# A multi-layer trunk kernel on one core: the first modulation and the first projection block taken feature tile by feature tile, with new ring slots and a new order of the adaLN steps

## The reference

```python
def layer(x, cond, l, p, ctx):
    mod = jnp.einsum('...d,de->...e', jax.nn.silu(cond), p['w_ada'][l]) + p['b_ada'][l]
    sh1, sc1, g1, sh2, sc2, g2 = jnp.split(mod.reshape(-1, 1, 6 * D_MODEL), 6, axis=-1)
    hn = rmsnorm(x, p['norm_mix'][l]) * (1.0 + sc1) + sh1
    mix, ctx_tensors = token_mixers(hn, l, p, ctx)     # proj = hn @ w_in[l]: attention, retention, HGRN2
    x = x + g1 * mix                                   # mix ends in @ w_out[l]
    hn = rmsnorm(x, p['norm_ffn'][l]) * (1.0 + sc2) + sh2
    x = x + g2 * moe(hn, l, p)                         # 16 experts, two picked for each token
    return x, ctx_tensors
```

## Time and profile before

| | |
|---|---|
| median of three runs | 952.8 us |
| the profiled run, and its span | 953.32 us, 951.5 us |
| TensorE busy | 920.2 us (97%) |
| VectorE, ScalarE, POOL busy | 431.9, 158.7, 63.7 us |
| adaLN loads | 48 of 1024 KB |
| projection loads | 28 of 1024 KB, 4 of 512 KB |

### The profile page before, as it was taken

One profiled execution on the slowest core, in us unless ns is written; L12 is line 12 of the kernel. 1 busy time (PEld: TensorE's weight loads), 2 busy tenths in 40 slices (PEclk: granted clock), 3 DMA queues, 4 the chain that ended last, 5 costly groups with the idle time before them and its releaser, 6 DMA issues.

```text
span 951.5 us, 13385 instructions
## 1 busy us (share of the span) xinstructions
PE 920.2 (97%) x5191; PEld 499.6 (53%) x5197; DVE 431.9 (45%) x780; ACT 158.7 (17%) x408; POOL 63.7 (7%) x96
## 2 busy tenths in 40 slices
PE   5999999999999999999999999999999999999997
PEld 2755575568553444344437556657864444443442
DVE  1385887742423122232145999876252321222223
ACT  2212024320210100010111211432021001000100
POOL 1112230020000000000000223000000000000001
PEclk9999999999999999999999999999999999999999
DMA  9996574675999999999996632601189999999993
GB/s 365 401 390 268 222 267 177 243 278 213 408 420 422 421 421 421 421 422 420 421 421 252 225 124 91 235 32 38 35 364 422 421 421 421 421 421 421 421 421 137
DMA packets 48430, 303.63 MB, mean 319 GB/s; under 512 B 7680, under 2 KB 7696, under 8 KB 14960
## 3 DMA queue, kind: packets, MB, share of 16 engines
q1 hardware_dynamic: 42368, 291.52, 75.2%
q0 software_dynamic: 2960, 8.63, 2.6%
q10 hardware_dynamic: 3040, 2.62, 0.8%
HBM read 300.10 MB, written 2.65 MB: 318 GB/s over the span
## 4 chain that ended last, share of the span: by engine, by line
PE 84%; DVE 9%; DMA 3%; ACT 2%; issue 1%; SPq 0%; DVEq 0%; ACTq 0%
PE ps L427 82%; PE ps L461 2%; DMA ring<-in_w_in 2%; ACT eP L1582 1%; DMA ring<-in_w_ada 1%; DVE fa L1263 1%; DVE rt L1057 1%; DVE eP L1361 1%; DVE stat L1057 1%; DVE xy L1257 1%; DVE eP L1359 1%; DVE hnT L1105 0%; DVE sq L1214 0%; DVE proj L1290 0%; DVE proj L1224 0%
## 5 line engine op out<-in xcount | busy, mean ns | idle before, releaser
L427 PE MATMUL ps<-ring,proj 128*64 128x512 f32 x1024 | 226.3, 595 | 1.0 <-ACT proj L1829 1.0
L427 PE MATMUL ps<-ring,hnT 128*128 128x512 f32 (+1 forms) x576 | 203.2, 505 | 2.3 <-issue 1.2
L427 PEld LDWEIGHTS ps<-ring,hnT 128*128 128x128 f32 x576 | 106.9, 191 | 75.9 <-issue 67.7
L427 PEld LDWEIGHTS ps<-ring,proj 128*64 128x64 f32 x1024 | 72.6, 137 | 132.8 <-issue 131.1
L427 PE MATMUL ps<-hnT,ring 128*64 128x128 f32 (+2 forms) x576 | 74.0, 342 | 2.9 <-DVE hnT L1105 1.6
L427 PEld LDWEIGHTS ps<-hnT,ring 128*64 128x64 f32 (+1 forms) x576 | 60.7, 160 | 13.9 <-issue 2.9
L427 PEld LDWEIGHTS ps<-proj,xs 128*128 128x128 f32 x512 | 58.4, 192 | 12.5 <-issue 11.4
L427 PE MATMUL ps<-proj 128*128 128x512 f32 x128 | 61.7, 607 | 0.0
L427 PE MATMUL ps<-proj,xs 128*128 128x128 f32 x512 | 61.4, 278 | 0.1
L1553 DVE COPY proj<-ps 128x512 f32<-128x512 f32 x16 | 11.1, 692 | 108.0 <-PE ps L427 108.0
L427 PE MATMUL ps<-ring,silT 128*32 128x512 f32 x384 | 48.8, 630 | 9.6 <-DVE silT L1073 6.9
(11 more groups left out here) (231 smaller groups left out, 920.9 us busy)
## 6 DMA issues: line engine op xcount, KB each, us to landing
ring<-in_w_gate SPq DMA_DIRECT2D x64, 1024.0 KB, 14.4
ring<-in_w_down SPq DMA_DIRECT2D x64, 1024.0 KB, 16.8
ring<-in_w_ada SPq DMA_DIRECT2D x48, 1024.0 KB, 8.6
ring<-in_w_in SPq DMA_DIRECT2D x28, 1024.0 KB, 8.5
eP<-in_w_up SPq DMA_DIRECT2D x16, 1024.0 KB, 15.8
wT<-in_w_up SPq DMA_DIRECT2D x16, 1024.0 KB, 17.9
fa<-in_w_up SPq DMA_DIRECT2D x16, 1024.0 KB, 17.7
xy<-in_w_up SPq DMA_DIRECT2D x16, 1024.0 KB, 19.1
```

What stands on the lines that cost most here:

```text
L427: ins = nc.tensor.matmul(*a, **k)
```

## The change

- The x part of layer 0's w_ada is laid out anew on the host as `ada_x`: load k now has all 1024 rows, but only the 128 shift and 128 scale columns of feature tile k. Its sums are 8 multiplies of 256 columns, spread over four groups of 32 array columns (rows i and i + 4 share one); ScalarE copies the four partial rows, two tiny multiplies with `pick` add and turn them, VectorE makes shift and scale of this tile and applies them for g = 0, ScalarE for g = 1.
- Block f of layer 0 is computed along with it: for each k, 8 multiplies of 256 columns, into both banks, right after the sums of feature k + 1.
- f's two halves are loaded to slots 8 and 9 and stand before adaLN loads 1 and 4 in SyncE's order. The ring begins at slot 2, so that block b lies in slots 0 and 1, the six steps behind it in 2 to 7, and i in 0 and 1.
- SyncE issues conditioning, tokens and constants ahead of the weights; POOL keeps the small parameters.
- `ADA_BEHIND` of layer 0 goes from (2, 3, 3, 3, 3, 2, 3, 2) to (0, 0, 2, 6, 6, 2, 3, 2). Of the six behind b, TensorE does three after the first and three after the third quarter of b, none at its end.
- The diagonals of layer 0 move from before a's last quarter to the start of block b.
- VectorE clamps both banks of f before the gates of bank 0 in layer 0. Fourteen zero multiplies open TensorE's program and no longer wait for the conditioning.

The diff, cut:

```diff
-ADA_BEHIND = ((2, 3, 3, 3, 3, 2, 3, 2), (0, 0, 0, 0, 0, 3, 0, 0))
+ADA_BEHIND = ((0, 0, 2, 6, 6, 2, 3, 2), (0, 0, 0, 0, 0, 3, 0, 0))
 AT_CHANGE = 5
+ROWS_AHEAD = (1, 4)
+FIRST_SLOT = 2
...
+            n_loads = [FIRST_SLOT]
...
+            for name, dst, src in (("cond_dma", condT[:], ap["cond"]), ("x_dma0", x[:, 0], ap["x_prompt"][0]),
+                                   ("begin_dma", C["begin"][:], ap["begin"]), ("x_dma1", x[:, 1], ap["x_sample"][0])):
+                sp.dma_start(dst, src).then_inc(S(name), 16)
+                led.made(name, (name, 0), 16)
...
                 if l == 0:
-                    for step in EARLY:
-                        load_ada(*step)
+                    for k in range(KC):
+                        if k in ROWS_AHEAD:
+                            r = ROWS_AHEAD.index(k)
+                            load_rows(*IN_BLOCKS[0], r, RING + r)
+                        load(flat_slot, ap["ada_x"][k])
...
-            pe.wait_ge(c.of("silT"), c.at("silT"))
...
-                if l == 0:
-                    b = claim_for_norm()
-                    for step in EARLY[0:5]:
-                        ada_step(*step)
-                        stream_zeros(b, 3)
-                    pe.wait_ge(c.of("begin_dma"), c.at("begin_dma"))
-                    normalized_group("hn1", "xn1", 0, first=b)
-                    normalized_group("hn1", "xn1", 1)
-                    for step in EARLY[5:]:
-                        ada_step(*step)
-                    modulation_by_feature(0, 0)
-                else:
+                def sums_of_feature(k):
+
+                    pe.wait_ge(S("bank1_free"), c.claim(1))
+                    s = slot()
+                    for i in range(KC):
+                        q = slice(32 * (i % 4), 32 * (i % 4) + 32)
+                        last = mm(ps[q, 1, 0:2 * P], silT[:, i, :], by_k(s, 2 * P)[:, i] if i < KH else flat_slot(s)[:, 2 * P * i:2 * P * (i + 1)], start=i < 4, stop=i >= 4)
+                        if i < KC - 1:
+                            pay(last)
+                    last.then_inc(c.fills(1, "ada", 0, "x", k), 1)
+                    owed.append(s)
+
+                def modulation_of_feature(k):
+
+                    pe.wait_ge(S("bank7_free"), c.claim(7))
+                    pe.wait_ge(c.of("modX", 0, 0, k), c.at("modX", 0, 0, k))
+                    for a in range(2):
+                        last = mm(ps[:, 7, NG * a:NG * (a + 1)], modX[:, 2 * P * (k % 2) + P * a:2 * P * (k % 2) + P * (a + 1)], C["pick"], start=True, stop=True)
+                        if not a:
+                            pay(last)
+                    last.then_inc(c.fills(7, "modT", 0, 0, k), 1)
...
+                def feature_of_first_block(k, ss, banks):
+
+                    for g in range(NG):
+                        pe.wait_ge(c.of(f"hn1S{g}", k), c.at(f"hn1S{g}", k))
+                    for p in range(2):
+                        for hl in range(2):
+                            for d in range(2):
+                                col = 64 * (2 * p + hl) + 256 * d
+                                last = mm(ps[64 * d:64 * d + 64, banks[p], 256 * hl:256 * (hl + 1)], by_k(ss[k // KH], 512)[:, k % KH, col:col + 64], hnT[:, k, :], start=False, stop=(k == KC - 1), skip_group_check=True)
+                                if k == KC - 1 and hl and d:
+                                    last.then_inc(c.fills(banks[p], "projP", "f", p), 1)
+                                else:
+                                    pay(last)
+
+                if l:
...
+                if l:
+                    b = next_bank()
+                    ss = open_block("f")
+                    by_head_and_group("f", 0, ss, b)
+                    by_head("f", 1, ss)
+                else:
+                    f_banks = [next_bank() for _ in range(2)]
+                    pe.wait_ge(c.of("zero", 0), c.at("zero", 0))
+                    stream_zeros(f_banks[0], 12)
+                    stream_zeros(f_banks[1], 2)
+                    pe.wait_ge(c.of("begin_dma", 0), c.at("begin_dma", 0))
+                    normalized_group("hn1", "xn1", 0, banks=(4, 5))
+                    pe.wait_ge(c.of("silT"), c.at("silT"))
+                    sums_of_feature(0)
+                    normalized_group("hn1", "xn1", 1, banks=(6, 0))
+                    ss = []
+                    for k in range(KC):
+                        modulation_of_feature(k)
+                        if k + 1 in ROWS_AHEAD:
+                            ss.append(slot(RING + len(ss)))
+                        if k + 1 < KC:
+                            sums_of_feature(k + 1)
+                        feature_of_first_block(k, ss, f_banks)
+                        if k % KH == KH - 1:
+                            owed.append(ss[k // KH])
...
-                diagonal(0)
-                diagonal(1)
+                if l:
+                    diagonal(0)
+                    diagonal(1)
...
+                if not l:
+                    diagonal(0)
+                    diagonal(1)
                 for g in range(NG):
                     b = by_token("b", g, 0, ss)
+                    if not l:
+                        ada_steps(3)
...
-                ada_behind("b")
+                ada_steps(ADA_BEHIND[l][3] % 6)
...
+            st(v.memset(zero, 0.0), "zero", 0)
...
-                    modulation_by_feature(0, 0)
                     for k in range(KC):
-                        ins = ts(hnT[:, k, 0:P], hnT[:, k, 0:P], modT[:, 1, k, 0:1], modT[:, 0, k, 0:1], ALU.mult, ALU.add)
-                        if k % KH == KH - 1:
-                            ins.then_inc(c.makes("hn1S0", k // KH), 1)
+                        dve.wait_ge(c.of("modT", 0, 0, k), c.at("modT", 0, 0, k))
+                        tt(modTs[:, 0, 0:2, k], ps[:, 7, 0:2 * NG].rearrange("p (a g) -> p a g", a=2), badaTs[:, 0, 0:2, one(k)].broadcast_to([P, 2, NG]), ALU.add).then_inc(c.freed(("modT", 0, 0, k)), 1)
+                        dve.wait_ge(S(c.last[0]), c.last_value())
+                        st(stt(out=modTs[:, 0, 1, k], in0=modTs[:, 0, 1, k], scalar=1.0, in1=nrmTs[:, 0, 0, one(k)].broadcast_to([P, NG]), op0=ALU.add, op1=ALU.mult), "modS", 0, 0, k)
+                        ts(hnT[:, k, 0:P], hnT[:, k, 0:P], modT[:, 1, k, 0:1], modT[:, 0, k, 0:1], ALU.mult, ALU.add).then_inc(c.makes("hn1S0", k), 1)
...
-                gates(0)
+                bounded(0)
+                if l:
+                    gates(0)
+                    bounded(1)
+                else:
+                    bounded(1)
+                    gates(0)
...
+                            if not l:
+                                acte.wait_ge(c.of(f"x_dma{g}", 0), c.at(f"x_dma{g}", 0))
...
+                    evac(("ada", 0, "x", 0), None, "modX", 0, 0, 0, fn=lambda src: nc.scalar.copy(modX[:, 0:2 * P], src[:, 0:2 * P]))
                     for h in range(2):
                         evac(("hn1T", 1, h), None, fn=lambda src: nc.scalar.copy(hnT[:, KH * h:KH * (h + 1), P:2 * P], src.rearrange("p (k t) -> p k t", k=KH)))
-                    modulation(0, "x", 0)
-                    acte.wait_ge(c.of("modS", 0, 0), c.at("modS", 0, 0))
                     for k in range(KC):
-                        ins = act_(hnT[:, k, P:2 * P], hnT[:, k, P:2 * P], AF.Identity, bias=modT[:, 0, k, 1:2], scale=modT[:, 1, k, 1:2])
-                        if k % KH == KH - 1:
-                            ins.then_inc(c.makes("hn1S1", k // KH), 1)
+                        acte.wait_ge(c.of("modS", 0, 0, k), c.at("modS", 0, 0, k))
+                        act_(hnT[:, k, P:2 * P], hnT[:, k, P:2 * P], AF.Identity, bias=modT[:, 0, k, 1:2], scale=modT[:, 1, k, 1:2]).then_inc(c.makes("hn1S1", k), 1)
+                        if k + 1 < KC:
+                            to = modX[:, 2 * P * ((k + 1) % 2):2 * P * ((k + 1) % 2) + 2 * P]
+                            evac(("ada", 0, "x", k + 1), None, "modX", 0, 0, k + 1, fn=lambda src: nc.scalar.copy(to, src[:, 0:2 * P]))
...
-            for name, lot in (("cond_dma", [(condT[:], ap["cond"])]),
-                              ("begin_dma", [(x[:, 0], ap["x_prompt"][0]), (x[:, 1], ap["x_sample"][0]), (C["begin"][:], ap["begin"])]),
-                              ("mod_dma", [(mods[:], ap["mods"])])):
-                for dst, src in lot:
-                    pool.dma_start(dst, src).then_inc(S(name), 16)
-                led.made(name, (name,), 16 * len(lot))
+            pool.dma_start(mods[:], ap["mods"]).then_inc(S("mod_dma"), 16)
+            led.made("mod_dma", ("mod_dma",), 16)
...
+    first = np.asarray(inputs["w_ada"])[0, :, 0:2 * D].reshape(P, KC, 2, KC, P)
+    out["ada_x"] = first.transpose(3, 0, 1, 2, 4).reshape(KC, P, KC * 2 * P)
```

53 lines of the change are left out of this document (26 added, 27 removed).

## The result

The change makes the kernel slower: 956.6 us median against 953.35 us for the kernel before on the same chip, ratio 1.0027, 95% interval 1.0014 to 1.0040. Forecast were 947.2 us and a range of 943.9 to 950.9. The profiled run took 955.85 us, its span is 954.0 (before 951.5). So in the spans 8.2 us are missing (-5.7 forecast, +2.5 measured). A table of one place after another in the two profiled runs shows where they went; negative is earlier than before.

What follows compares the result with a forecast made beforehand. The prediction took layer 0 as a load-bound head of 33 us, then a TensorE-bound body. Its terms, 7.7 + 1.2 - 3.2 = 5.7 us, rounded down to 5.6, took the median from 952.8 to 947.2 us; range 943.9 to 950.9.

Steps and rivals of the forecast that it cites:

- Head, the start: Layer 0's head: adaLN load k=4 lands at 24.4 us, and the time to block f's end counts from there.
- Head, the step: Feature loop: 3.45 us of TensorE time per step, 16.5 us from k=4's landing, so block f ends at 40.9.
- Break before a: Ahead of block a: TensorE's break of 1.19 us goes, as a's weights land by about 41, wanted at 48.
- VectorE before the diagonals: Between f's end and the diagonals: VectorE done at +22.2 us, TensorE there at +22.8, slack 0.6 us.
- The wait before i: Before block i: TensorE waits 3.2 us for i's second half, which needs the slot of b's; bounds 2.9 and 9.3.
- rival 2: Feature loop or after the wait before i: one or two half-clock stretches, 1.6 us each, time 948.8 to 950.4; chance 0.24.
- No further wait: Behind block i: later loads arrive in time, r's second half by 122 us, wanted at 123.
- From 127.92 on the order is unchanged and TensorE-bound or tied to TensorE, so the shift is kept to the end.: From layer 0's first transposes to the end: the whole gain of 5.7 us is kept.
- The sign: Whole kernel: 5.7 us faster; chance 0.82 faster by more than 1.9 us, 0.12 within that, 0.06 slower.
- a late VectorE: Before the diagonals: VectorE becomes the bound, each us late costs one; chance 0.08, shared with a queue ahead of i's load.
- a queue ahead of i's load: Before block i: i's load meets a full queue, 6 us more, time 953.2; chance 0.08, shared with a late VectorE.
- a feature loop at half clock: Layer 0's head: clock stays at half throughout, f ends at 53.5, total 6.8 us slower, 959.6; chance 0.05.

Runs made afterwards that it cites:

- split356: Changed kernel with layer 0's adaLN steps behind a, b, i at 3, 5, 6 instead of 2, 6, 6; 951.5 us, ratio 0.9976.
- warm_i: Changed kernel with 28 bf16 multiplies of a constant in front of the wait before block i in layer 0; 955.5 us, ratio 1.0015.
- before_shift: Kernel before with fourteen idle one-column copies near the start of ScalarE's program; 957.9 us, ratio 1.0046.
- after_shift: Changed kernel with six idle one-column copies near the start of ScalarE's program; 959.3 us, ratio 1.0053.
- after_store: Changed kernel with layer 0's o_k and o_v stores moved behind block s's weight copies, swish and squares on ScalarE; 953.8 us, ratio 0.9996.
- router_zeros: split356 with nine more zero multiplies by TensorE in layer 0's router; 950.3 us, ratio 0.9970.
- split356_store: split356 with layer 0's o_k and o_v stores moved behind block s's weight copies, swish and squares on ScalarE; 948.2 us, ratio 0.9941.
- before_store: Kernel before with layer 0's o_k and o_v stores moved behind block s's weight copies, swish and squares on ScalarE; 953.4 us, ratio 0.9999.
- before_at4: Kernel before with four instead of five adaLN steps between the layers; ratio 0.9997.

## Why the prediction was wrong, step by step

- **Head, the start.** Mis-sized by 1.9 us. The forecast let TensorE keep up with the loads until k=4 and counted from its landing, 24.4. In the trace TensorE is behind from the sums of k=1 at 15.69 on, and comes to those of k=4 at 26.33. The load itself lands at 26.0, 1.6 us later than forecast (8.13 MiB costed at 2.49 us each from the old order), but by then it no longer decides.
- **Head, the step.** 3.45 forecast, 3.61 measured: f 1.88 rather than 1.8, sums with the gap behind them 1.2 rather than 1.15, turning 0.54 rather than 0.5. From the sums of k=4 to f's end that is 17.5 rather than 16.5, 1.0 us. Together block f ends at 43.86, not 40.9. That TensorE's own work and not the loads sets the step was right.
- **Break before a, VectorE before the diagonals.** Right: the break is gone, and the wait for VectorE is 0.24 us.
- **The wait before i.** Right: 3.2 forecast, 3.39 measured; split356 removes it. Missing from the sum was the half clock behind it, 1.61 us. The forecast held it as rival 2 and gave it 0.24, although it named that wait as longer than any in the body. That it follows from the wait is shown by warm_i. "No further wait" behind i held by 0.3 us only: r's second half was to land by 122 and landed at 127.6, since it too waits for a slot, and warm_i waits 2.20 us for it.
- **"From 127.92 on the order is unchanged and TensorE-bound or tied to TensorE, so the shift is kept to the end."** This is the step that failed. In the two profiled runs -0.94 us is kept until 185; then come +2.2 at block s and +1.2 in the head of layer 1. The first comes from ScalarE's program, which the change lengthens by its tile by tile copies: the store became the 193rd recorded instruction rather than the 178th, and its issue takes 2.21 us rather than 0.38. That the count decides is shown by before_shift and after_shift; that a fetch of instructions holds the issue up is only inferred. after_store against the change gives its price, about 3 us, with intervals that just touch; before_shift, on the other kernel, gives 0.46%. The second has its cause in the load stream, which had been left out of the forecast altogether: between w_gate and layer 1 the end is set by 262.7 to 264.3 us of loads, so what TensorE does or saves there is not seen, save that a longer idle wait before the block brings half clock.
- **The sign.** The sum was -5.7. Measured: 3.0 us missing at f's end (the break is as forecast), 0.2 and 1.6 at block i, then 2.2 and 1.2 behind it; that is +8.2 and makes +2.5. The first three alone would have given 952.0 us, no change; what came behind 127.92 made it slower. No rival had the failed step. The 18% for same or slower named a late VectorE, a queue ahead of i's load and a feature loop at half clock, none of which cost over 0.3 us in the profiled run; "unforeseen waits" stood there without a mechanism. (One stretch at half clock in the loop does occur in some executions of the changed order, router_zeros and after_shift among them.)
- **The size of what is to be had** was right, in part by chance. The forecast was 947.2 of 952.8, or 0.9941, and split356_store measures 0.9941: it lacks the wait of 3.4 us that the forecast held, and its f ends 3 us later than the forecast had it.

Open stay what makes one execution run at half clock near 187 us without a wait and another of the same program not; how the transfer and the slow issue hang together; and whether after_shift's copies have a part in its slow head.

## What to carry to other kernels

"The rest is unchanged, so the shift is kept" has to be argued like any other term: ask for each stage what sets its end (here a saturated load stream, whose start and length are all that counts), and what the change moves besides time. A longer program on one engine can make a DMA issue far behind the edit slow; a DMA issue on a compute engine should stand behind the work that others wait for, where it costs nothing (before_store). Give each new wait on TensorE a stretch at half clock as a likely second term: behind the wait at i it was there in four of four traces and cost 1.6 to 3 us. And read more than one trace before a difference of 1 us between two of them is given a cause.

## What the runs showed of the hardware

- The issue of the store out_o_k on ScalarE takes 0.38 us, or 1.94 to 2.33 where it is ScalarE's 192nd or 193rd recorded instruction: in six traces, in before_shift by design. In each of the six a transfer of kind instruction begins 0.43 to 0.70 us into it. That this transfer fetches ScalarE's own code is inferred from its moving with the count of ScalarE's instructions. A copy at the same place is not slowed (0.59 us in split356_store), and a transfer inside the issue of another store did not slow it (0.60 us there).
- Fourteen idle copies of 0.1 us near the start cost 0.46% (0.28 to 0.64), and the trace shows them at work 180 us later.
- Half clock behind an idle wait of TensorE, by traces. Wait of 3.2 to 3.4 us at block i: four of four. In the head of layer 1: behind 1.89, 1.99 (twice), 2.01, 2.06 and 2.23 us, and not behind 0.70, 0.92, 1.20, 1.39 and 1.61. Not behind 2.20 us at block r in warm_i.
- The same program has such a stretch in one execution and not in another (the quarter of block s: 4.85 us in the profiled run of the kernel before, 3.70 in before_at4, whose program is the same up to there).
- More work can be free or better: in router_zeros nine more multiplies inside the load stream, by which the turns begin 1.5 us later, cost nothing, the wait ahead of layer 1's block was 0.70 us, and no half clock followed, where it did in the change (1.99), split356_store (2.06) and before_shift (2.23).
